# Residual of the delta inversion: b as two fp16 parts times the fp16 x, in place of fp32 b times a widened x

## The chip, the cores and the metric

The kernel runs on one core of a Trainium2 chip. The metric is the device time of one execution in microseconds. Three runs of the kernel before gave 3141.36, 3142.63 and 3150.59 us, so its median is 3142.63 us.

## The reference

One layer of a hybrid diffusion backbone over 1024 latent and 256 context tokens with 1024 channels: a modulation, a combined input projection, a bidirectional gated DeltaNet with 8 heads of 128 channels, a windowed attention, a merge of both branches, and a convolutional FFN. The change touches the DeltaNet alone. Its reference, cut to the part in question, is

```
gc = cumsum(g in the chunk)
decay = where(i >= j, exp(gc_i - gc_j), 0)
kk = k @ k.T
a_mat = where(i > j, beta_i * kk * decay, 0)
sol = triangular_solve(a_mat, [v * beta, k * beta * exp(gc)], lower=True, unit_diagonal=True)
```

and then a scan over the chunks. The solve is with the matrix I + a_mat. The kernel uses chunks of 128 tokens in place of 64, so each head has 10 chunks (8 latent, 2 of context) in 2 directions: 20 triangular matrices of 128x128.

## The kernel before, in words

`delta_net` runs 8 heads one after another. Every engine has its own program: a prologue, a loop over heads 0 to 6 with `fill` true, and the last head, written out with `fill` false. Nothing orders the engines but the counted semaphores (`Count`), and each engine takes its instructions in the order in which they are written.

A head goes through four stages:

- **Prepare** (`pe_prepare`, `act_body`, `dve_body`, `pool_body`). Tiles of two chunks in both directions (`bt` = 0 to 4, 128x512 numbers each) go through in turn: GpSimd masks g (`masked_g`), TensorE sums it and makes k @ k.T, ScalarE takes the exponential, VectorE multiplies into `bf` (b_full, fp32; L1666), GpSimd sets the diagonal of `bf` to 1 (L1806), and ScalarE rounds `bf` to fp16 as `b_h` (b_half, L1511). So b is I + a_mat in fp32, and b_h is its fp16 rounding.
- **Inversion** (`pe_inverse`, first loop). 7 levels of merging blocks of doubled size, 4 steps each, all in fp16: the products with `b_h` (L1303) are masked by VectorE with the level masks in `mats` (L1678, L1680) and give `x_h` (x_half), an approximate inverse, and `y_h` (y_half), its transpose.
- **Residual** (`pe_inverse`, second loop, L1343 to L1366). One refinement makes up for the fp16 of the inversion. For each `bt`, TensorE multiplies b with x in fp32: 4 matmuls of `bf` (L1351) with `x_f` (x_full), which is x_h widened to fp32 by GpSimd for bt 0, 2, 4 (L1819) and by ScalarE for bt 1, 3 (L1524). VectorE takes -2048 times the product plus 2048 times I as the fp16 residual `e_h` (L1692), TensorE multiplies it with y_h (4 matmuls, L1364), and VectorE adds 1/2048 of this to y_h and overwrites `bf` with it (L1700), which is the inverse that the chain uses. The residual tiles have two buffers. VectorE's order is e(0), e(1), inverse(0), e(2), inverse(1), e(3), inverse(2), e(4), inverse(3), inverse(4); TensorE's is product(0), product(1), second(0), product(2), second(1), and so on.
- **Chain** (`pe_chain`). The scan over 10 chunks, forward and backward. In heads 0 to 6, TensorE fills the waits between its small matmuls with the projections of the next head (`pe_group`, L1202), whose weight tiles GpSimd splits into a high and a low part (`pool_split`: L176 and L183).

GpSimd's order in a head: column copy (L1777), `masked_g` and `units`, five diagonals (L1806) with the other masks between them, the clearing of `o_acc` (L1812), two splits (the next head's k and v weights), the three widenings (L1819), then `pool_lines`, which waits for the end of the residual stage, and two more splits.

`decays` makes the columns of all heads in the prologue; `per_head` holds 6 kinds (`NK`) of 20 columns per head, which are copied to `col` at the start of a head. `x_f` lies over the first half of the region that held `conv_out`.

Of the kernel before, what the change touches and what calls it, by code (L numbers as in the profile page):

```python
# [15 lines left out]
P = 128  # L16
# [50 lines left out]
def constants():  # L67
    r, c = np.arange(P)[:, None], np.arange(P)[None, :]
    rot = np.zeros((P, P), np.float32)
    for base in (0, 64):  # L70
        for d in range(32):
            rot[base + 32 + d, base + d] = -1.0
            rot[base + d, base + 32 + d] = 1.0
    mats = [r == c, r >= 0, rot, c < r, c > r, c <= r, c >= r, NEG * (c < r), NEG * (c > r)]
    for level in range(LEVELS):
        s = 1 << level
        m = (r // (2 * s) == c // (2 * s)) & ((r // s) % 2 == 1) & ((c // s) % 2 == 0)
        unit = 1.0 * (r == c) if level == 0 else 0.0
        even = (np.arange(P) // s) % 2 == 0
        mats.append(np.concatenate([(unit - m)[:, even], (unit - m.T)[:, ~even]], 1))  # L80
    mats = np.stack([np.broadcast_to(m, (P, P)) for m in mats], 1).astype(np.float32)
    inv_freq = (np.float32(10000.0) ** (-np.arange(32, dtype=np.float32) / np.float32(32))).astype(np.float32)
    t = np.arange(SEQ)
    ang_r = (t // GRID_W).astype(np.float32)[None, :] * inv_freq[:, None]
    ang_c = (t % GRID_W).astype(np.float32)[None, :] * inv_freq[:, None]
    ang = np.concatenate([ang_r, ang_r, ang_c, ang_c], 0)
    return mats, np.stack([np.cos(ang), np.sin(ang)], 1).astype(np.float32)
# [878 lines left out]
K_G, K_BETA, K_EG, K_NEG_EG, K_BETA_REST, K_TOTAL = range(6)  # L966
NK = 6

def decays(core, per_head, at, ps, out):  # L970
# [50 lines left out]
    def vector_last(dve):  # L1021
        dve.wait_ge(s, 4)
        chain(dve, dve.tensor_tensor(ex[:, :, 1, :], ex[:, :, 1, :], beta[:, :, :], ALU.mult))
        chain(dve, dve.tensor_scalar(m[:, :, :], ex[:, :, 0, :], -1.0, None, ALU.mult))
        for kind, src in ((K_G, g[:, :, :]), (K_BETA, beta[:, :, :]), (K_EG, ex[:, :, 0, :]),
                          (K_NEG_EG, m[:, :, :]), (K_BETA_REST, ex[:, :, 1, :]), (K_TOTAL, ex[:, :, 2, :])):
            for di in range(2):
                dve.tensor_copy(per_head[:, :, kind, :, di].rearrange("p h c -> p c h"),
                                src[:, :, di * HEADS:(di + 1) * HEADS]).then_inc(out, 1)
        dve.wait_ge(out, 2 * NK)  # L1030

# [41 lines left out]
E_SCALE = 2048.0  # L1073
# [9 lines left out]
def delta_net(core, d):  # L1083
# [5 lines left out]
    with ExitStack() as st:  # L1089
# [38 lines left out]
        x_f = place("x_full", [P, NCH, 2, P], 0, F32)  # L1128
# [36 lines left out]
        xev, yac, xfa, osq = C("x_copied"), C("y_copied_act"), C("x_widened_act"), C("o_std")  # L1165
# [9 lines left out]
        xfp, unit = C("x_widened_pool"), C("x_and_y_units")  # L1175
# [92 lines left out]
        def pe_inverse(pe, h):  # L1268
# [73 lines left out]
            for bt in range(BT + 1):  # L1342
                if bt < BT:  # L1343
                    if bt % 2:
                        xfa.wait(pe, h * 2 + bt // 2 + 1)
                    else:
                        xfp.wait(pe, h * 3 + bt // 2 + 1)
                    ed.wait(pe, h * 5 + bt - 1)
                    for m in range(4):
                        c, di = 2 * bt + m // 2, m % 2  # L1350
                        mm = pe.matmul(bank[4 + bt % 2][:, m * P:(m + 1) * P], bf[:, c, di, :],  # L1351
                                       x_f[:, c, di, :], start=True, stop=True)
                    mm.then_inc(rd_.sem, 1)
# [139 lines left out]
        def act_body(act, h, fill):  # L1493
# [28 lines left out]
            xev.wait(act, h * MSTEPS + MSTEPS)  # L1522
            for bt in (1, 3):
                act.activation(flat(x_f, bt), flat(x_h, bt), ACT.Copy).then_inc(xfa.sem, 1)  # L1524
# [15 lines left out]
        def scalar(act):  # L1540
            for c in (evac, sil, sqd, stdc, tka, kqc, dct, bhd, xev, yac, xfa, osq):
                c.open(act)
# [109 lines left out]
        def dve_body(dve, h, fill):  # L1652
# [5 lines left out]
            for bt in range(BT):  # L1658
# [5 lines left out]
                for n in range(4):  # L1664
                    c, di = 2 * bt + n // 2, n % 2
                    ins = dve.scalar_tensor_tensor(out=bf[:, c, di, :], in0=bank[6 + bt % 2][:, (n // 2) * P:(n // 2 + 1) * P],  # L1666
                                                   scalar=col[:, K_BETA, c, di:di + 1], in1=dec[bt % 2][:, n // 2, di, :],
# [18 lines left out]
            for bt in range(BT + 1):  # L1686
                if bt < BT:
# [6 lines left out]
                                             scalar=-E_SCALE, in1=id_e[:, :].unsqueeze(1).broadcast_to([P, 4, P]),  # L1694
# [79 lines left out]
        def pool_body(pool, h, fill):  # L1774
# [28 lines left out]
            for bt in range(BT):  # L1803
                bqd.wait(pool, h * 5 + bt + 1)
                pool.sem_inc(turns, 1)
                pool.affine_select(flat(bf, bt), flat(bf, bt), pattern=[[0, 4], [1, P]], compare_op=ALU.not_equal,  # L1806
                                   fill=1.0, base=0, channel_multiplier=-1).then_inc(bfd.sem, 1)
                if bt + 2 < BT:
                    masked_g(bt + 2)
            pool.wait_ge(ystored, h * 16 + 16)  # L1810
# [5 lines left out]
            for bt in (0, 2, 4):  # L1816
                xev.wait(pool, h * MSTEPS + MSTEPS - (2 if bt == 0 else 0))
                pool.sem_inc(turns, 1)
                pool.tensor_copy(flat(x_f, bt), flat(x_h, bt)).then_inc(xfp.sem, 1)  # L1819
# [6 lines left out]
        def gpsimd(pool):  # L1826
            for c in (colc, tapc, padz, bfd, gld, dgd, xfp, unit, oz):
# [488 lines left out]
```

## Time and profile before

| | |
|---|---|
| median of three runs | 3142.63 us |
| the profiled execution | 3137.65 us, of which its span is 3135.8 us |
| TensorE matmuls busy | 2777.6 us (89% of the span) |
| VectorE busy | 1459.5 us (47%) |
| ScalarE busy | 775.3 us (25%) |
| GpSimd busy | 676.8 us (22%) |
| mean granted TensorE clock | 0.916 |
| the eight heads of the DeltaNet | from about 908 us to 2060 us of the span |

### The profile page before, as it was taken

How to read it: one execution, taken by the hardware profiler on the slowest of the kernel's cores; microseconds unless marked ns; L12 is line 12 of the kernel's file. 1: busy time of each engine (PE TensorE's matmuls, PEld its weight loads, DVE VectorE, ACT ScalarE, POOL GpSimd, SP SyncE). 2: the span in 40 equal slices, each digit the busy share in tenths (PEclk: the TensorE clock that was granted, in tenths of full speed). 3: DMA queues.
4: the chain of work that ended last, by engine and by line, in shares of the span. 5: the costliest groups of instructions: out<-in, count | busy, mean ns of one | idle time of the engine just before them, and what ended most of it. 6: DMA issues, size and time to landing. Idle time of an engine off the chain costs nothing. (4 is left out here: it accounts for less than half of the span.)

```text
span 3135.8 us, 45853 instructions
## 1 busy us (share of the span) xinstructions
PE 2777.6 (89%) x16872; PEld 2333.4 (74%) x16872; DVE 1459.5 (47%) x2531; ACT 775.3 (25%) x1386; POOL 676.8 (22%) x505
## 2 busy tenths in 40 slices
PE   8599999899889897988889897699686999997999
PEld 7476888778778786877778786578465888886877
DVE  1474444310436666656656666522114555555232
ACT  1421333210132514233242514110113121122010
POOL 0242000033231312122231312033112333331111
PEclk7799988899979899999989898799797999998999
DMA  4110112131100101000000100132321111111433
GB/s 190 56 33 7 61 67 95 73 109 66 54 8 7 35 1 36 14 23 22 15 28 8 35 1 8 66 116 87 121 100 47 47 53 47 47 47 60 127 124 98
DMA packets 41783, 175.69 MB, mean 56 GB/s; under 512 B 4624, under 2 KB 4880, under 8 KB 39696
## 3 DMA queue, kind: packets, MB, share of 16 engines
q1 hardware_dynamic: 39312, 169.19, 15.5%
q10 hardware_dynamic: 2304, 4.20, 0.3%
q8 instruction: 114, 1.87, 0.2%
q14 instruction: 53, 0.43, 0.0%
HBM read 148.20 MB, written 25.17 MB: 55 GB/s over the span
## 5 line engine op out<-in xcount | busy, mean ns | idle before, releaser
L193 PE MATMUL ps_up<-h_hi,up_w_hi 128*128 128x512 f32 x704 | 274.7, 390 | 37.4 <-POOL up_w_lo L183 37.4
L194 PE MATMUL ps_up<-h_lo,up_w_hi 128*128 128x512 f32 x704 | 274.4, 390 | 0.0
L195 PE MATMUL ps_up<-h_hi,up_w_lo 128*128 128x512 f32 x704 | 274.3, 390 | 0.0
L1202 PE MATMUL dn_bank<-h_hi,dn_w_hi 128*128 128x512 f32 (+1 forms) x640 | 245.4, 384 | 12.4 <-POOL dn_w_lo L183 12.4
L1202 PE MATMUL dn_bank<-h_hi,dn_w_lo 128*128 128x512 f32 (+1 forms) x640 | 245.7, 384 | 0.0
L1202 PE MATMUL dn_bank<-h_lo,dn_w_hi 128*128 128x512 f32 (+1 forms) x640 | 245.1, 383 | 0.0
L2072 DVE TENSOR_SCALAR ffn_u<-ffn_pad,vectors 128x1024 f32<-128x1024 f32 x44 | 105.3, 2394 | 230.7 <-ACT ffn_pad L2052 230.7
L193 PEld LDWEIGHTS ps_up<-h_hi,up_w_hi 128*128 128x128 f32 x704 | 132.5, 188 | 65.9 <-issue 38.2
L2141 PE MATMUL ps_down<-act_hi,down_w_hi 128*128 128x512 f32 x352 | 139.1, 395 | 24.5 <-DVE act_lo L2180 24.5
L194 PEld LDWEIGHTS ps_up<-h_lo,up_w_hi 128*128 128x128 f32 x704 | 132.6, 188 | 27.5
L195 PEld LDWEIGHTS ps_up<-h_hi,up_w_lo 128*128 128x128 f32 x704 | 132.4, 188 | 27.5
L1567 DVE SCALAR_TENSOR_TENSOR conv_out<-conv_in,head_taps,conv_out 128x1284 f32<-128x1284 f32 (+1 forms) x96 | 148.2, 1544 | 0.4
L1202 PEld LDWEIGHTS dn_bank<-h_hi,dn_w_hi 128*128 128x128 f32 x640 | 122.6, 192 | 29.7 <-POOL dn_w_lo L183 12.8
L1454 ACT ACTIVATE conv_in<-dn_bank 128x512 f32<-128x512 f32 (+1 forms) x64 | 34.9, 545 | 427.5 <-PE dn_bank L1202 421.3
L2142 PE MATMUL ps_down<-act_lo,down_w_hi 128*128 128x512 f32 x352 | 138.8, 394 | 0.0
L2143 PE MATMUL ps_down<-act_hi,down_w_lo 128*128 128x512 f32 x352 | 138.4, 393 | 0.0
L1202 PEld LDWEIGHTS dn_bank<-h_lo,dn_w_hi 128*128 128x128 f32 x640 | 122.7, 192 | 17.2
L1202 PEld LDWEIGHTS dn_bank<-h_hi,dn_w_lo 128*128 128x128 f32 x640 | 122.5, 191 | 17.0
L183 DVE TENSOR_TENSOR down_w_lo<-down_w_raw,down_w_hi 128x1408 fp32r<-128x1408 f32 x32 | 52.1, 1627 | 161.2 <-POOL down_w_hi L176 161.2
L176 POOL CAST up_w_hi<-up_w_raw 128x1024 fp32r<-128x1024 f32 x44 | 45.7, 1039 | 371.4 <-PE ps_up L195 311.3
L2076 DVE SCALAR_TENSOR_TENSOR ffn_u<-ffn_pad,vectors,ffn_u 128x1024 f32<-128x1024 f32 x88 | 113.0, 1285 | 12.8 <-DVE ffn_u L2076 0.2
L2052 ACT ACTIVATE ffn_pad<-ps_up 128x1024 f32<-128x1024 f32 x44 | 45.3, 1029 | 285.0 <-PE ps_up L195 284.9
(313 smaller groups left out, 6726.1 us busy)
## 6 DMA issues: line engine op xcount, KB each, us to landing
up_w_raw<-in_w_up SPq DMA_DIRECT2D x44, 512.0 KB, 3.3
down_w_raw<-in_w_down SPq DMA_DIRECT2D x32, 704.0 KB, 4.2
late_w_ada<-in_w_ada SPq DMA_DIRECT2D x8, 2048.0 KB, 9.7
dn_w_raw<-in_w_dn SPq DMA_DIRECT2D x32, 512.0 KB, 3.4
w_ada<-in_w_ada SPq DMA_DIRECT2D x4, 2048.0 KB, 12.7
at_w_raw<-in_w_mg_at SPq DMA_DIRECT2D x16, 512.0 KB, 4.2
dnm_w_raw<-in_w_mg_dn SPq DMA_DIRECT2D x16, 512.0 KB, 5.4
x_in<-in_xT SPq DMA_DIRECT2D x8, 640.0 KB, 10.0
```

The source lines that it names most:

```text
L176: pool.tensor_copy(self.hi[j][:, :, :], self.raw[j][:, :, :]).then_inc(self.hi_made, 1)
L183: eng.tensor_tensor(self.lo[j][:, :, :], self.raw[j][:, :, :], self.hi[j][:, :, :].bitcast(F32), ALU.subtract).then_inc(self.split, 1)
L193: pe.matmul(out, self.hi[j][:, k, :], xh, start=(k == 0), stop=False)
L194: pe.matmul(out, self.hi[j][:, k, :], xl, start=False, stop=False)
L195: mm = pe.matmul(out, self.lo[j][:, k, :], xh, start=False, stop=(k == self.kt - 1))
L1202: mm = pe.matmul(bank[4 + s % 3][:, 0:n], wt[:, k, :], x[:, k, t0:t0 + n], start=(k == 0 and v == 0), stop=(k == KT - 1 and v == 2))
L1567: ins = dve.scalar_tensor_tensor(out=dst, in0=src[:, j:j + n], scalar=taps[:, tile_at(tile), j:j + 1], in1=dst, op0=ALU.mult, op1=ALU.add)
L2072: ins = dve.tensor_scalar(u[:, s, :], src, tap(0), vec[:, bass.ds(m + s * FT + V_CONVB, 1)], ALU.mult, ALU.add)
L2076: ins = dve.scalar_tensor_tensor(out=u[:, s, :], in0=src, scalar=tap(n), in1=u[:, s, :], op0=ALU.mult, op1=ALU.add)
L2141: pe.matmul(ps[j][:, :], w.hi[part][:, k, :], hi, start=(kk == 0), stop=False)
L2142: pe.matmul(ps[j][:, :], w.hi[part][:, k, :], lo, start=False, stop=False)
L2143: mm = pe.matmul(ps[j][:, :], w.lo[part][:, k, :], hi, start=False, stop=(kk == FT - 1))
```

## The change

The fp32 product of the residual is replaced by two fp16 products that are added up in PSUM. b is scaled by 2048 (`E_SCALE`) as it is made: `decays` adds a seventh kind of column, `K_BETA_E` = 2048 beta, L1666 uses it in place of beta, and GpSimd sets the diagonal to 2048. `b_h` is then the fp16 rounding of the scaled b, and a new tile `b_l` (b_rest_half) holds in fp16 what the rounding left; GpSimd makes it by a subtraction for each `bt`, after the five diagonals and ahead of the clearing of `o_acc`. The level masks are divided by 2048, so that the inversion yields the same x and y. TensorE multiplies `b_h` and `b_l` with `x_h` (8 matmuls in fp16 for each `bt`, where 4 in fp32 were), and the factor of the residual on VectorE is -1 in place of -2048. `x_f` and its five widenings are gone.

```diff
-        mats.append(np.concatenate([(unit - m)[:, even], (unit - m.T)[:, ~even]], 1))
+        mats.append(np.concatenate([(unit - m)[:, even], (unit - m.T)[:, ~even]], 1) / E_SCALE)
...
-NK = 6
+K_G, K_BETA, K_EG, K_NEG_EG, K_BETA_REST, K_TOTAL, K_BETA_E = range(7)
+NK = 7
+E_SCALE = 2048.0
...
+        chain(dve, dve.tensor_scalar(e[:, :, :], beta[:, :, :], E_SCALE, None, ALU.mult))
         for kind, src in ((K_G, g[:, :, :]), (K_BETA, beta[:, :, :]), (K_EG, ex[:, :, 0, :]),
-                          (K_NEG_EG, m[:, :, :]), (K_BETA_REST, ex[:, :, 1, :]), (K_TOTAL, ex[:, :, 2, :])):
+                          (K_NEG_EG, m[:, :, :]), (K_BETA_REST, ex[:, :, 1, :]), (K_TOTAL, ex[:, :, 2, :]),
+                          (K_BETA_E, e[:, :, :])):
...
-        x_f = place("x_full", [P, NCH, 2, P], 0, F32)
+        b_l = place("b_rest_half", [P, NCH, 2, P], 0, F16)
...
-                    if bt % 2:
-                        xfa.wait(pe, h * 2 + bt // 2 + 1)
-                    else:
-                        xfp.wait(pe, h * 3 + bt // 2 + 1)
+                    xev.wait(pe, h * MSTEPS + MSTEPS - (2 if bt < 2 else 0))
+                    bld.wait(pe, h * 5 + bt + 1)
                     ed.wait(pe, h * 5 + bt - 1)
                     for m in range(4):
                         c, di = 2 * bt + m // 2, m % 2
-                        mm = pe.matmul(bank[4 + bt % 2][:, m * P:(m + 1) * P], bf[:, c, di, :],
-                                       x_f[:, c, di, :], start=True, stop=True)
+                        pe.matmul(bank[4 + bt % 2][:, m * P:(m + 1) * P], b_h[:, c, di, :],
+                                  x_h[:, c, di, :], start=True, stop=False)
+                        mm = pe.matmul(bank[4 + bt % 2][:, m * P:(m + 1) * P], b_l[:, c, di, :],
+                                       x_h[:, c, di, :], start=False, stop=True)
...
-            xev.wait(act, h * MSTEPS + MSTEPS)
-            for bt in (1, 3):
-                act.activation(flat(x_f, bt), flat(x_h, bt), ACT.Copy).then_inc(xfa.sem, 1)
...
-                                                   scalar=col[:, K_BETA, c, di:di + 1], in1=dec[bt % 2][:, n // 2, di, :],
+                                                   scalar=col[:, K_BETA_E, c, di:di + 1], in1=dec[bt % 2][:, n // 2, di, :],
...
-                                             scalar=-E_SCALE, in1=id_e[:, :].unsqueeze(1).broadcast_to([P, 4, P]),
+                                             scalar=-1.0, in1=id_e[:, :].unsqueeze(1).broadcast_to([P, 4, P]),
...
-                                   fill=1.0, base=0, channel_multiplier=-1).then_inc(bfd.sem, 1)
+                                   fill=E_SCALE, base=0, channel_multiplier=-1).then_inc(bfd.sem, 1)
...
+            kqc.wait(pool, h + 1)
+            for bt in range(BT):
+                bhd.wait(pool, h * 5 + bt + 1)
+                pool.sem_inc(turns, 1)
+                pool.tensor_tensor(flat(b_l, bt), flat(bf, bt), flat(b_h, bt), ALU.subtract).then_inc(bld.sem, 1)
...
-            for bt in (0, 2, 4):
-                xev.wait(pool, h * MSTEPS + MSTEPS - (2 if bt == 0 else 0))
-                pool.sem_inc(turns, 1)
-                pool.tensor_copy(flat(x_f, bt), flat(x_h, bt)).then_inc(xfp.sem, 1)
```

GpSimd's rows from the last two diagonals of a head to the first rows that follow the residual stage, before (dn_w_hi and dn_w_lo are the split weights, L1761 belongs to `pool_lines`):

```order
L1806 AFFINE_SELECT b_full<-b_full 128x512
L1810 ISA
L1812 MEMSET o_acc 128x1024
...
L176 CAST dn_w_hi<-dn_w_raw_4609 128x1024
...
L183 TENSOR_TENSOR dn_w_lo<-dn_w_raw_4609,dn_w_hi 128x1024
...
L176 CAST dn_w_hi<-dn_w_raw_4610 128x1024
...
L183 TENSOR_TENSOR dn_w_lo<-dn_w_raw_4610,dn_w_hi 128x1024
...
L1819 CAST x_full<-x_half 128x512
...
L1819 CAST x_full<-x_half 128x512 x2
```

The same place of the changed kernel:

```order
L1805 AFFINE_SELECT b_full<-b_full 128x512
L1813 TENSOR_TENSOR b_rest_half<-b_full,b_half 128x512 x5
L1814 ISA
L1816 MEMSET o_acc 128x1024
...
L176 CAST dn_w_hi<-dn_w_raw_4609 128x1024
...
L183 TENSOR_TENSOR dn_w_lo<-dn_w_raw_4609,dn_w_hi 128x1024
...
L176 CAST dn_w_hi<-dn_w_raw_4610 128x1024
...
L183 TENSOR_TENSOR dn_w_lo<-dn_w_raw_4610,dn_w_hi 128x1024
```

Five subtractions stand ahead of the clearing and of both splits; the three widenings behind the splits are gone.

TensorE's rows at the start of the residual stage of a head in the loop, before (the first line is the end of the inversion):

```order
L1332 MATMUL dn_bank<-identity_half,x_half 128x64 x10
L129 REGISTER_ALU
L1351 MATMUL dn_bank<-x_full,b_full 128x128 x4
L129 REGISTER_ALU
L1351 MATMUL dn_bank<-x_full,b_full 128x128 x4
L129 REGISTER_ALU
L1364 MATMUL dn_bank<-y_half,residual_half 128x128 x4
```

The same place of the changed kernel; the pair of its second and third rows comes eight times:

```order
L1334 MATMUL dn_bank<-identity_half,x_half 128x64 x10
L1351 MATMUL dn_bank<-x_half,b_half 128x128
L1353 MATMUL dn_bank<-x_half,b_rest_half 128x128
...
L129 REGISTER_ALU
L1366 MATMUL dn_bank<-y_half,residual_half 128x128 x4
```

8 fp32 matmuls became 16 in fp16, and two register operations ahead of the products are gone, since the waits need fewer computed values.

## Rows read from the trace of the kernel before

**Rows 1.** The page's first part: busy us, share of the span, instructions.

```profile
PE 2777.6 (89%) x16872; PEld 2333.4 (74%) x16872; DVE 1459.5 (47%) x2531; ACT 775.3 (25%) x1386; POOL 676.8 (22%) x505
```

**Rows 2.** Stretches: length; busy us of PE, PEld, DVE, ACT, POOL; PEclk; DMA share; GB/s.

```profile
955.05:963.30 8.25, 6.31 (x60) 5.77 (x60) 6.92 (x13) 0.67 (x2) 0.64 (x2) 1.00 0.01 2
1104.00:1165.00 61.00, 60.38 (x368) 53.62 (x369) 36.87 (x100) 10.85 (x14) 7.19 (x8) 0.99 0.00 1
```

**Rows 3.** Timeline, residual stage of head 1: start us, us, engine, line, operation [idle before].

```profile
1095.63 2.02 PE L1351 MATMUL dn_bank<-x_full,b_full 128*128 128x128 f32 x16
...
1096.96 0.69 DVE L1692 SCALAR_TENSOR_TENSOR residual_half<-dn_bank,identity_e_scale 128x512 f16<-128x512 f32 x1 [0.71 <-PE dn_bank L1351]
1097.84 0.69 DVE L1692 SCALAR_TENSOR_TENSOR residual_half<-dn_bank,identity_e_scale 128x512 f16<-128x512 f32 x1 [0.19 <-PE dn_bank L1351]
...
1097.99 0.38 PE L1364 MATMUL dn_bank<-y_half,residual_half 128*128 128x128 f16 x4 [0.35 <-DVE residual_half L1692]
...
1098.45 0.68 DVE L1700 SCALAR_TENSOR_TENSOR b_full<-dn_bank,y_half 128x512 f32<-128x512 f32 x1
...
1099.42 0.69 DVE L1692 SCALAR_TENSOR_TENSOR residual_half<-dn_bank,identity_e_scale 128x512 f16<-128x512 f32 x1 [0.29 <-issue]
1100.03 0.68 DVE L1700 SCALAR_TENSOR_TENSOR b_full<-dn_bank,y_half 128x512 f32<-128x512 f32 x1
...
1102.42 1.28 DVE L1700 SCALAR_TENSOR_TENSOR b_full<-dn_bank,y_half 128x512 f32<-128x512 f32 x2
...
1103.89 0.71 PE L1376 MATMUL dn_bank<-state,k_t 128*128 128x128 f32 x4 [0.94 <-DVE state L1608]
...
1104.36 0.48 PE L1202 MATMUL dn_bank<-h_hi,dn_w_hi 128*128 128x512 f32 x1
```

**Rows 4.** The same, first and last rows of head 4, and rows of head 7.

```profile
1519.18 2.02 PE L1351 MATMUL dn_bank<-x_full,b_full 128*128 128x128 f32 x16
...
1526.14 1.28 DVE L1700 SCALAR_TENSOR_TENSOR b_full<-dn_bank,y_half 128x512 f32<-128x512 f32 x2
...
1946.10 2.03 PE L1351 MATMUL dn_bank<-x_full,b_full 128*128 128x128 f32 x16
...
1947.34 0.69 DVE L1692 SCALAR_TENSOR_TENSOR residual_half<-dn_bank,identity_e_scale 128x512 f16<-128x512 f32 x1 [0.55 <-PE dn_bank L1351]
...
1952.52 1.27 DVE L1700 SCALAR_TENSOR_TENSOR b_full<-dn_bank,y_half 128x512 f32<-128x512 f32 x2
```

**Rows 5.** Groups by shape, 800 to 2000 us: busy us, mean ns | idle before.

```profile
L183 POOL TENSOR_TENSOR dn_w_lo<-dn_w_raw,dn_w_hi 128x1024 fp32r<-128x1024 f32 x32 | 77.0, 2407 | 2.6
...
L1786 POOL TENSOR_TENSOR g_masked<-constants,head_columns 128x512 f32<-128x512 f32 x40 | 41.2, 1039 | 1.4 <-POOL head_columns L1777 1.4
...
L1364 PE MATMUL dn_bank<-y_half,residual_half 128*128 128x128 f16 x160 | 15.5, 219 | 8.1 <-DVE residual_half L1692 8.1
```

**Rows 6.** Timeline, GpSimd in head 1: last diagonal, last split, first widening.

```profile
1071.75 0.63 POOL L1806 TENSOR_SCALAR_AFFINE_SELECT b_full<-b_full 128x512 f32<-128x512 f32 x1 [2.32 <-DVE b_full L1666]
...
1077.76 2.36 POOL L183 TENSOR_TENSOR dn_w_lo<-dn_w_raw,dn_w_hi 128x1024 fp32r<-128x1024 f32 x1
...
1093.64 0.61 POOL L1819 CAST x_full<-x_half 128x512 f32<-128x512 f16 x1 [13.53 <-ACT x_half L1516]
```

**Rows 7.** Timeline, VectorE in the prologue: columns of the decays.

```profile
908.52 0.24 DVE L1024 TENSOR_SCALAR decay_m<-decay_exps 128x160 f32<-128x160 f32 x1
...
909.69 0.57 DVE L1028 COPY per_head_columns<-decay_exps 128x80 f32<-128x80 f32 x4
```

**Rows 8.** Stretches in head 1 (first three) and head 7, columns as in rows 2.

```profile
1071.39:1074.80 3.41, 1.76 (x40) 1.42 (x40) 2.31 (x6) 1.17 (x2) 2.96 (x4) 1.00 0.00 0
1074.80:1078.21 3.41, 3.15 (x49) 2.75 (x48) 2.34 (x6) 1.53 (x4) 3.33 (x3) 0.50 0.13 29
1100.50:1103.90 3.40, 1.79 (x21) 1.44 (x18) 3.40 (x8) 0.00 (x0) 0.00 (x0) 1.00 0.00 0
1955.43:1972.50 17.07, 15.74 (x58) 13.00 (x58) 9.77 (x33) 0.00 (x0) 0.00 (x0) 0.50 0.01 1
```

More of the change, by code:

```diff
@@ L962, in attention @@
     merge_stage(core, "at", core.y_dram, d["w_mg_at"], core.merged_dram)
-K_G, K_BETA, K_EG, K_NEG_EG, K_BETA_REST, K_TOTAL = range(6)
-NK = 6
+K_G, K_BETA, K_EG, K_NEG_EG, K_BETA_REST, K_TOTAL, K_BETA_E = range(7)
+NK = 7
+E_SCALE = 2048.0
 def decays(core, per_head, at, ps, out):
@@ L1072 @@
 YHALF = STEPS // 2
-E_SCALE = 2048.0
 ORDER = [list(range(XCH, NCH)) + list(range(XCH)), list(range(NCH - 1, XCH - 1, -1)) + list(range(XCH - 1, -1, -1))]
@@ L1164, in delta_net @@
         tka, kqc, dct, bhd = C("tok_act"), C("kq_copied"), C("decay"), C("b_rounded")
-        xev, yac, xfa, osq = C("x_copied"), C("y_copied_act"), C("x_widened_act"), C("o_std")
+        xev, yac, osq = C("x_copied"), C("y_copied_act"), C("o_std")
         qsd, ovr = C("q_sums_copied"), C("o_var")
@@ L1174, in delta_net @@
         colc, tapc, padz, bfd, oz = C("columns"), C("taps"), C("pad_zeroed"), C("b_with_i"), C("o_zeroed")
-        xfp, unit = C("x_widened_pool"), C("x_and_y_units")
+        bld, unit = C("b_rest"), C("x_and_y_units")
         gld, dgd = C("g_masked"), C("k_rstd_diag")
@@ L1540, in scalar @@
         def scalar(act):
-            for c in (evac, sil, sqd, stdc, tka, kqc, dct, bhd, xev, yac, xfa, osq):
+            for c in (evac, sil, sqd, stdc, tka, kqc, dct, bhd, xev, yac, osq):
                 c.open(act)
@@ L1826, in gpsimd @@
         def gpsimd(pool):
-            for c in (colc, tapc, padz, bfd, gld, dgd, xfp, unit, oz):
+            for c in (colc, tapc, padz, bfd, gld, dgd, bld, unit, oz):
                 c.open(pool)
```

## The prediction

> **What bounds the kernel now.** I began with the page's first part: TensorE's matmuls are busy for 89% of the span, every other engine for less than half [rows 1]. The change touches one stage of each of eight heads, so the next view is the stretches around it. In the chain, which takes about 61 of a head's 141 us (heads 1 to 4 start their stages at 1095.63 and 1519.18), TensorE is busy for 60.38 of 61.00 us at a granted clock of 0.99: it is the bound there, and whatever the stage ahead of it saves reaches the end in full, since the chain's first matmul waits for the last inverse. In the residual stage nothing is full: PE 6.31, VectorE 6.92 of 8.25 us, ScalarE and GpSimd next to nothing, clock 1.00 [rows 2]; the other seven stages are alike.
>
> The timeline of one such stage shows who waits for whom [rows 3]. TensorE starts product(0) and product(1), 16 records, at 1095.63. VectorE's e(0) starts 1.33 us later, e(1) at 1097.84. e(0) is over at 1097.65, and second(0) starts 0.34 us after that; inverse(0) starts 0.46 us behind second(0). e(2) at 1099.42 is still late. From there VectorE starts an operation every 0.60 or 0.61 us (1099.42, 1100.03), ends at 1103.70 and waits for nothing. So the stage has two parts: a start in which VectorE waits for fp32 products, and a steady part of 0.60 us per VectorE operation, which TensorE doesn't set. From 1095.63 to 1103.70 it is 8.07 us. Five heads (0, 1, 3, 5, 6) have this length within 0.01 us, heads 2 and 4 have 8.22 and 8.24, since second(0) starts 0.16 us later there, and the last has 7.69 [rows 4].
>
> **The change part by part.** *The products.* Before: 16 records in 2.02 us; with 0.22 us for a matmul by itself [rows 5] that is (2.02 - 0.22) / 15 = 0.12 us each, and product(0), 8 records, is done 7 x 0.12 + 0.22 = 1.06 us after its start. e(0) follows 0.27 us later (1.33 - 1.06). After: also 8 matmuls, in fp16. Four such matmuls (second(0)) take 0.38 us [rows 3], one takes 0.219 [rows 5], so they follow each other by (0.38 - 0.22) / 3 = 0.054 us. product(0) is done after 7 x 0.054 + 0.22 = 0.60, and e(0) starts at 0.60 + 0.27 = 0.87 us. Then, from the start of the stage: e(1) at 1.47 (product(1) is done at 1.03); e(0) over at 1.56; second(0) at 1.90; inverse(0) at 2.36. product(2) is issued 0.22 us behind the start of second(0), at 2.12, and allows e(2) at 2.99. Six more starts of 0.60 (inverse 1, e 3, inverse 2, e 4, inverse 3, inverse 4) give 6.59, and the last lasts 0.68: 7.27 us. That is 0.80 us less than 8.07. Heads 2 and 4 keep their 0.16 us, so they save the same; the last head begins e(0) at 1.24 - 0.46 = 0.78, has a short wait for second(0) and comes to 6.86 for 7.69, 0.83 less. Sum: 8 x 0.80 = 6.5 us saved. Although TensorE's work on the products falls by half (5 x 8 x (0.12 - 0.054) = 2.6 us a head), only 0.8 of it is on the path: the rest stands beside VectorE's 0.60 us steps.
>
> The trace has no chain of fp16 matmuls that alternates two weights into one PSUM bank. Bounds: if they went at the fp32 records' 0.12 us, nothing is saved; if every wait of VectorE in the start vanished, the stage would be 0.87 + 9 x 0.60 + 0.68 = 6.95 us, 1.12 us a head, 9 us in all. I take 6.5, near the upper end, because second(0) is the same shape and type. The Trainium skill (TensorE: Matmul & The Clock Gate, Back-to-back issue gap) gives about 81 ns per load-and-matmul pair at 128 columns; by it the products would be done 0.2 us later in each head and the sum would be 4.9 instead of 6.5, while the row has 54.
>
> *The widenings.* Five casts of some 0.6 us on two engines go. TensorE waited for none of them: GpSimd's first ran at 1093.64 [rows 6], two microseconds ahead of product(0), which itself follows the end of the inversion. Nothing is saved. The waits in their place (last x_half, rest made) are older still; two register operations ahead of the products go and one wait is added: 0, with 0.05 us a head either way.
>
> *The subtractions on GpSimd.* Five of 128x512, which no row shows. g_masked, 128x512 from two inputs, takes 1.04 us; the split's 128x1024 takes 2.41, or 1.2 us for half [rows 5]. I take 1.1 each, 5.5 us; between nearly nothing (0.6 each, as the casts) and 2.4 each, 12 us. They start behind the last diagonal and its rounding, at about 1072.9, so the rests are ready by 1079 (by 1085 at worst), and product(0) comes at 1095. Queued behind them: the clearing of o_acc and two splits, which ended at 1080.12 and will end at 1085.6 (1092 at worst); the chain's first use of those weights is at 1104.36 [rows 3]. GpSimd idled 13.53 us there [rows 6]. Cost: nothing; the idle stretch is the cover, and beyond 24 us of subtractions it would be gone. They now run beside the inversion's masks on VectorE, as the splits did already.
>
> *The prologue.* One more 128x160 operation, 0.24 us, and two more copies of 0.57 / 4 = 0.14 us [rows 7], 0.5 us once, ahead of GpSimd's first column copy, with TensorE's transposes beside it: between 0 and 0.5, I take 0.2. The column copy of each head grows by a sixth, beside transposes too: 0. VectorE's other operations change a constant only.
>
> *The clock.* This is the term that I can't read off. TensorE does less in the stage: per tile 8 x 0.12 + 4 x 0.054 = 1.18 us of matmuls before, 12 x 0.054 = 0.65 after; over the stage 5.9 of 8.07 us (73%) becomes 3.2 of 7.27 (45%). Granted clock falls in this kernel where TensorE is thinly occupied though never idle for long: in head 1, after 3.41 us with 1.76 busy, it was 0.50 for 3.41 us; the last 3.40 us of the residual stage had 1.79 busy, mostly fp32 columns, and the clock held [rows 8]. In the last head, whose chain has no filling work, it fell right behind the stage and stayed at 0.50 for 17 us. So the residual stage is near the edge, and its second half (one product, two seconds and the wait for the last inverse) goes down to less than such stretches had. A fall comes a little after, when TensorE should run the chain's dense matmuls. A stretch of 3.41 us at 1.2 instead of 2.4 GHz costs half of itself, 1.7 us, if all of it is dense; some of it will lie over the end of the stage, and I take 1.3. Where the stage lies against these spells differs from head to head, so I expect it in four of the seven filled heads: 4 x 1.3 = 5.2 us given back, with ends 0 and 7 x 1.7 = 12.
>
> The Trainium skill, same page, What's actually happening, says that the "default state is throttled, and activity releases the throttle", and its account of kernels that lose the clock is of waits with an idle TensorE. The change adds no such wait, and by that account the clock would hold; the rows of this case show falls without idleness.
>
> Sum: -6.5 + 0.2 + 5.2 = -1.1 us on 3137.65, the profiled execution. That execution is 5 us under the median of 3142.63; on the median it gives 3141.5 us.
>
> **The rivals.** *The clock holds* in all heads. For it: it held in all eight stages before; against it: rows 8. Then -6.5 + 0.2 = -6.3, 3136.3 us.
>
> *The clock falls in every filled head*, at the chain's start: slower than before. For it: the thin second half of the stage; against it: the spells don't begin at the same point of every head. 7 x 1.7 = 12 against 6.3 saved: +5.6, 3148.2 us. It decides from 5 heads at 1.3 us on; beyond +9.4 us it would need second spells behind the first, for which the dense chain leaves little room.
>
> *The products aren't what VectorE waits for*, or the alternating weights slow the fp16 matmuls to the fp32 pace: the change doesn't do what it says for the time. Against it: the 0.71 us that VectorE idles before e(0) ends with L1351. Then 0 to +0.5, 3142.9 us.
>
> **How the numbers follow.** Forecast 0.45, clock holds 0.30, clock falls everywhere 0.13, no gain 0.12. About 0.3% (9.4 us) is what a measurement of this kernel can tell from no change, and all four lie inside it: the largest saving that I can build is 9 us, the largest loss 6. Faster by more than 0.3% needs the upper bound or luck with spells elsewhere in the heads, whose places all shift: 0.12. Slower by more than 0.3%: 0.07. Within: 0.81. Range: from the clock that holds with a little more, 3133, to the fall in every head, 3149; the three runs of before are themselves 9 us apart.
>
> **What would show it.** The residual stage from first product to last inverse: 7.27 us in heads 0, 1, 3, 5, 6, with e(0) at 0.87 and VectorE's starts 0.60 apart from e(2) on. b_rest_half about 1.1 us each, over well before the stage, and no wait of PE for POOL. PEclk in the 4 us behind the stage: 0.50 for a spell in about four of heads 0 to 6. Wrong would be: a stage of over 7.6 us; no spell in any head, or one in all seven; a wait for a split at the chain's start; longer masks (L1680) on VectorE beside the subtractions.

## The result: 0.3% slower, outside the predicted range

| | before | changed |
|---|---|---|
| median of 5 runs each | 3142.08 us (3138.76 to 3150.59) | 3153.18 us (3147.00 to 3157.43) |
| ratio, 95% interval | | 1.003 (1.0016 to 1.0044) |
| profiled execution, its span | 3137.65, 3135.8 us | 3147.00, 3145.2 us |

Forecast were 3141.5 us and a range of 3133 to 3149. A second measurement of the same changed kernel (12 runs, 20 of before) gave 3153.19 against 3146.58, 1.0017 (1.0007 to 1.0028): slower again, by 6.6 us. The two intervals together put the loss between 2 and 14 us.

The page's first part of the changed kernel, as in [rows 1]. TensorE's busy time fell by only 2 us: by 17 in the eight residual stages (50.5 to 33.5), while in the chains it rose by 11 (591.7 to 602.7), where the same matmuls ran at a lower clock. GpSimd's rose by 29.

```profile
PE 2775.5 (88%) x16872; PEld 2325.2 (74%) x16872; DVE 1459.5 (46%) x2534; ACT 767.6 (24%) x1370; POOL 705.5 (22%) x521
```

The residual stage of head 1 from the first product on, and 61 us of its chain (columns as in [rows 2]). The stage was 8.07 us and is 7.15; TensorE's busy time in it was 6.31 and is 4.20, and its clock held. In the chain TensorE is busy for the same 60.38 us, but at a mean clock of 0.97 where it was 0.99.

```profile
1097.21:1104.36 7.15, 4.20 (x63) 3.36 (x60) 6.66 (x12) 0.00 (x0) 0.00 (x0) 1.00 0.01 2
1105.00:1166.00 61.00, 60.38 (x363) 53.40 (x362) 35.59 (x99) 9.38 (x12) 6.86 (x4) 0.97 0.00 1
```

The timeline of that stage: TensorE's first two products (start us, us), VectorE's operations, and the matmuls behind them. They answer to [rows 3].

```profile
1097.21 0.22 PE L1351 MATMUL dn_bank<-x_half,b_half 128*128 128x128 f16 x1
1097.27 0.22 PE L1353 MATMUL dn_bank<-x_half,b_rest_half 128*128 128x128 f16 x1
```
```profile
1098.02 1.29 DVE L1691 SCALAR_TENSOR_TENSOR residual_half<-dn_bank,identity_e_scale 128x512 f16<-128x512 f32 x2 [0.20 <-PE dn_bank L1353]
1099.48 0.69 DVE L1699 SCALAR_TENSOR_TENSOR b_full<-dn_bank,y_half 128x512 f32<-128x512 f32 x1 [0.17 <-PE dn_bank L1366]
1100.09 0.68 DVE L1691 SCALAR_TENSOR_TENSOR residual_half<-dn_bank,identity_e_scale 128x512 f16<-128x512 f32 x1
...
1103.07 1.28 DVE L1699 SCALAR_TENSOR_TENSOR b_full<-dn_bank,y_half 128x512 f32<-128x512 f32 x2
```
```profile
1099.06 0.38 PE L1366 MATMUL dn_bank<-y_half,residual_half 128*128 128x128 f16 x4 [0.79 <-DVE residual_half L1691]
...
1103.22 0.40 PE L1366 MATMUL dn_bank<-y_half,residual_half 128*128 128x128 f16 x4 [0.80 <-DVE residual_half L1691]
1104.55 0.60 PE L1378 MATMUL dn_bank<-state,k_t 128*128 128x128 f32 x3 [0.94 <-DVE state L1607]
```

e(0) starts 0.81 us behind the first product (1098.02 - 1097.21), against 1.33 before; from e(2) at 1100.09 on VectorE runs back to back. The wait in front of e(0) has gone from 0.71 to 0.20 us.

GpSimd in head 1, to set beside [rows 6]: the five subtractions are over at 1079.71, the second split at 1087.45, and GpSimd then idles for 17 us. Forecast were 1079 and 1085.6, the split being 1.9 us later than that without anybody waiting; 1.6 us of it is that the whole head lies later (first product 1097.21 instead of 1095.63). Behind the prologue, which has two copies and one operation more [rows 7], head 0's column copy begins at 912.36 instead of 910.68.

```profile
1074.09 5.62 POOL L1813 TENSOR_TENSOR b_rest_half<-b_full,b_half 128x512 f16<-128x512 f32 x5
...
1085.08 2.37 POOL L183 TENSOR_TENSOR dn_w_lo<-dn_w_raw,dn_w_hi 128x1024 fp32r<-128x1024 f32 x1
1104.59 0.18 POOL L1760 MEMSET conv_in<- 128x4 f32 x3 [17.14 <-DVE b_full L1699]
```

**Where the time went.** I divided each head at four marks: GpSimd's column copy, VectorE's first x_half, the first product, the end of the last inverse. "Filled" heads are heads 0 to 6, whose chains hold projections of the next head. A fall is a change of the granted clock from 1.00 to 0.50 (2.4 to 1.2 GHz), and a spell is the time it stays there. "Low" is the time at a granted clock of 0.50, worked out for each stretch as twice its length times (1 - PEclk). Sums over eight heads of the profiled executions, us:

| | to first x_half (low) | to product(0) (low) | residual stage | chain (low) | end of head 7 |
|---|---|---|---|---|---|
| before | 198.4 (82) | 189.5 (30) | 64.5 | 643.3 (68) | 2006.4 |
| changed | 200.6 (90) | 189.7 (30) | 56.8 | 655.2 (91) | 2014.6 |
| changed, again | 198.3 (88) | 191.1 (37) | 57.3 | 660.5 (107) | 2026.5 |

The residual stage gave back 7.7 us. The chain, whose instructions the change doesn't touch, took 11.9 more: 13.4 more in the filled heads, 1.5 less in the last (52.58 to 51.04). The part to the first x_half took 2.2 more, the way to the first head 1.7, the inversion 0.2. Together -7.7 + 11.9 + 2.2 + 1.7 + 0.2 = 8.3 of the span's 9.4 us.

The chain's loss stands in the clock. These are the 10 us behind the residual stage, heads 0 to 7 of the changed kernel, then heads 0 and 1 of before, where all seven filled heads read 1.00 (length; busy us of PE, PEld, DVE, ACT, POOL; PEclk; DMA share; GB/s):

```profile
963.67:973.67 10.00, 9.80 (x53) 8.38 (x54) 3.28 (x14) 0.60 (x1) 0.37 (x4) 1.00 0.01 2
1104.36:1114.36 10.00, 9.81 (x44) 8.31 (x45) 3.23 (x12) 0.60 (x1) 0.37 (x4) 0.83 0.01 2
1246.24:1256.24 10.00, 9.82 (x36) 8.25 (x37) 2.70 (x10) 0.00 (x0) 0.37 (x4) 0.68 0.01 2
1389.60:1399.60 10.00, 9.83 (x36) 8.27 (x37) 2.69 (x10) 0.00 (x0) 0.37 (x4) 0.68 0.01 2
1532.70:1542.70 10.00, 9.81 (x45) 8.39 (x46) 3.32 (x12) 0.60 (x1) 0.38 (x4) 0.84 0.01 2
...
1963.00:1973.00 10.00, 8.30 (x31) 6.68 (x31) 6.51 (x21) 0.00 (x0) 0.00 (x0) 0.65 0.00 0
```
```profile
963.12:973.12 10.00, 9.80 (x53) 8.42 (x54) 3.33 (x14) 0.60 (x1) 0.37 (x4) 1.00 0.01 2
1103.70:1113.70 10.00, 9.81 (x53) 8.46 (x54) 3.35 (x13) 0.60 (x1) 0.37 (x4) 1.00 0.01 2
```

PEclk 0.83 over 10 us is 3.4 us at 1.2 GHz, 0.68 is 6.4 us. Six of seven filled heads have a fall there, two of them a double one (the spell lasts twice as long): 3.4 + 6.4 + 6.4 + 3.2 + 3.4 + 3.0 = 25.8 us low, of which half is lost where TensorE is the bound: up to 12.9 us. In head 2 the timeline of TensorE and the stretches show it record by record:

```profile
1245.21 0.28 PE L1366 MATMUL dn_bank<-y_half,residual_half 128*128 128x128 f16 x2
1246.42 1.23 PE L1378 MATMUL dn_bank<-state,k_t 128*128 128x128 f32 x4 [0.94 <-DVE state L1607]
...
1247.87 0.63 PE L1204 MATMUL dn_bank<-h_lo,dn_w_hi 128*128 128x512 f32 x1
1248.29 0.63 PE L1204 MATMUL dn_bank<-h_hi,dn_w_lo 128*128 128x512 f32 x1
```
```profile
1242.00:1245.40 3.40, 1.98 (x28) 1.37 (x25) 3.40 (x7) 0.00 (x0) 0.00 (x0) 1.00 0.02 5
1245.40:1248.80 3.40, 2.46 (x10) 2.09 (x9) 1.80 (x6) 0.00 (x0) 0.37 (x4) 0.55 0.00 0
1248.80:1252.20 3.40, 3.40 (x12) 2.82 (x11) 0.68 (x3) 0.00 (x0) 0.00 (x0) 0.50 0.00 0
1252.20:1255.60 3.40, 3.40 (x18) 2.82 (x17) 1.05 (x4) 0.00 (x0) 0.00 (x0) 0.95 0.00 0
```

The four fp32 matmuls that take 0.71 us in [rows 3] take 1.23 here, and the 512-column ones follow each other by 0.42 us (1248.29 - 1247.87) instead of 0.23. The clock goes to 0.50 while TensorE waits 0.94 us for the last inverse, and stays there through a whole stretch in which TensorE is busy for 3.40 of 3.40 us. Head 3 does the same, to the hundredth (1392.50 to 1395.90: busy 3.40, clock 0.50).

What TensorE did just before is in the last 3.40 us of head 1's stage, before and changed:

```profile
1100.30:1103.70 3.40, 1.98 (x22) 1.61 (x21) 3.40 (x7) 0.00 (x0) 0.00 (x0) 1.00 0.00 0
```
```profile
1100.96:1104.36 3.40, 1.50 (x20) 0.98 (x18) 3.40 (x7) 0.00 (x0) 0.00 (x0) 1.00 0.00 0
```

Its work there fell from 1.98 to 1.50 us, and its longest wait stayed at 0.94.

### The profile page after: what moved, and what is told of

Same layout as the page of the kernel before. It is cut to its first block and busy times, and to the rows that moved or that the text cites. A ratio compares the mean times of both kernels' runs of the same rounds, so it can differ in the third digit from the quotient of the medians.

```text
span 3145.2 us, 45851 instructions
## 1 busy us (share of the span) xinstructions
PE 2775.5 (88%) x16872; PEld 2325.2 (74%) x16872; DVE 1459.5 (46%) x2534; ACT 767.6 (24%) x1370; POOL 705.5 (22%) x521
## 6 DMA issues: line engine op xcount, KB each, us to landing
late_w_ada<-in_w_ada SPq DMA_DIRECT2D x8, 2048.0 KB, 10.5
```

## The experiments

Theory A: the clock's falls behind the stage cost what the chain lost, and they come because TensorE does too little in the stage. Rival B: the subtractions on GpSimd slow something. Rival C: the slower result is scatter between executions. In the diffs below lines of context are left out. Ratios are to the kernel before, measured together with each experiment, with 95% intervals.

**1. The changed kernel again, no edit.**

> The changed kernel as it is, on the chip and in the rounds of the next three. Both theories: 8 to 12 us slower than before, as measured. Its profile is a second look at where the granted clock falls: in the first one TensorE's clock was at 0.50 over the start of the chain in six of the seven filled heads (twice for some 6.8 us instead of 3.4). If that belongs to the change, five or more of seven show it again; if it was chance, two to four do.

Measured: 3153.19 us (3147.99 to 3162.57), 1.0017 (1.0007 to 1.0028), 6.6 us by the medians where 8 to 12 was expected. The clock fell behind the stage in seven of seven filled heads, in two of them twice. Heads 0, 1 and 3 of its trace, in the 10 us behind the stage:

```profile
970.60:980.60 10.00, 9.80 (x36) 8.26 (x37) 2.72 (x11) 0.00 (x0) 0.37 (x4) 0.69 0.01 2
1113.72:1123.72 10.00, 9.81 (x45) 8.38 (x46) 3.32 (x12) 0.60 (x1) 0.37 (x4) 0.84 0.01 2
...
1400.60:1410.60 10.00, 9.81 (x36) 8.28 (x37) 2.72 (x10) 0.00 (x0) 0.38 (x4) 0.68 0.00 0
```

Rival C falls: both measurements are slower and the falls repeat.

**2. and 3. Idle matmuls in the residual stage of the changed kernel.** They write a PSUM bank that nobody reads then; the result is unchanged. Number 2 issues 48 a head (8 behind each of products 1 to 4, at the last turn and at the end), number 3 only the 24 last of these.

```diff
+            def idle_work(k, end=False):
+                for i in range(k):
+                    a, b = (core.id_h[:, :],) * 2 if end else (b_h[:, i % 4, 0, :], x_h[:, i % 4, 0, :])
+                    pe.matmul(bank[3][:, (i % 4) * P:(i % 4 + 1) * P], a, b, start=True, stop=True)
...
                     mm.then_inc(rd_.sem, 1)
+                    if bt in (4,):          # number 2: (1, 2, 3, 4)
+                        idle_work(8)
                 if bt >= 1:
+                    if bt == BT:
+                        idle_work(8)
...
                     mm.then_inc(y2d.sem, 1)
+            idle_work(8, end=True)
```

> The changed kernel with TensorE work that nobody reads: 48 fp16 matmuls per head into a free PSUM bank, 8 behind each of products 1 to 4, 8 ahead of the last second product and 8 behind it, in TensorE's waits for VectorE. That is 2.6 us a head, as much as the change took from TensorE. Theory A (the thinner residual stage makes the granted clock fall at the chain's start, and that is the loss): the clock holds there in all heads, the residual stage stays within 0.4 us of its 7.14 us, and the kernel is 4 to 8 us faster than before (ratio 0.9975 to 0.9987). Theory B (the loss comes from elsewhere: subtractions on GpSimd, prologue, a shift of the heads): it stays 8 us slower or gets slower still by the added work.

> As the one before, but only at the end of the stage: 8 idle matmuls behind product 4, 8 ahead of the last second product and 8 behind it, 24 per head. Theory A, if the last 3 us of the stage decide: as good as the one with 48, clock held in all or all but one head, 4 to 8 us faster than before. If the whole stage counts: spells in some heads, between the two. Theory B: 8 us slower as the changed kernel.

Measured: 3134.82 us, 0.9958 (0.9945 to 0.9972), and 3133.46 us, 0.9954 (0.994 to 0.9969). Work that computes nothing makes the changed kernel 18 and 20 us faster than it was when measured together with them (3153.19). Behind the stage no head of number 3 has a fall; heads 0, 1 and 7:

```profile
967.02:977.02 10.00, 9.80 (x53) 8.40 (x54) 3.31 (x14) 0.60 (x1) 0.37 (x4) 1.00 0.01 2
1107.45:1117.45 10.00, 9.80 (x53) 8.41 (x54) 3.29 (x14) 0.60 (x1) 0.37 (x4) 1.00 0.01 2
...
1951.10:1961.10 10.00, 8.50 (x45) 6.15 (x46) 7.41 (x25) 0.00 (x0) 0.00 (x0) 1.00 0.01 2
```

Its residual stages sum to 56.7 us, as in the changed kernel, and its chains to 635.5 (33 low) against 655.2 (91 low). Against before the stage gives 7.8 us and the last head's chain 5.6 (52.58 to 46.94): together 13.4; the rest of the heads about cancels (filled chains -2.3, the part to the first x_half +2.5, inversion -0.4). The medians differ by 13.1. The spans of the two profiled executions differ by 6.9 only: number 3's is 5.1 us longer ahead of the heads (first column copy at 915.77 instead of 910.68) and 1.4 behind them. So theory A accounts for what the changed kernel had lost: against it number 3 differs in the idle matmuls alone, its stage is as long, and its chains are 19.7 us shorter. It is more than I had expected, since the last head gains as well.

**4. Less work still.** Only the product with b's high part is left; b's low part is missing from the residual.

```diff
-                        pe.matmul(bank[4 + bt % 2][:, m * P:(m + 1) * P], b_h[:, c, di, :],
-                                  x_h[:, c, di, :], start=True, stop=False)
-                        mm = pe.matmul(bank[4 + bt % 2][:, m * P:(m + 1) * P], b_l[:, c, di, :],
-                                       x_h[:, c, di, :], start=False, stop=True)
+                        mm = pe.matmul(bank[4 + bt % 2][:, m * P:(m + 1) * P], b_h[:, c, di, :],
+                                       x_h[:, c, di, :], start=True, stop=True)
```

> The changed kernel without the matmuls with b_rest_half (4 fp16 matmuls a tile in place of 8; the residual then lacks b's low part); the subtractions on GpSimd stay. TensorE does still less in the stage. Theory A: the stage is 0.2 to 0.3 us shorter a head, and the clock falls at the chain's start in all seven filled heads, more often for two spells: 0 to 5 us slower than the changed kernel though work was taken out. Theory B: 2 us faster than the changed kernel.

Measured: 3156.09 us, 1.0024 (1.001 to 1.0038). The stages sum to 55.4 us, another 1.4 less, and the chains to 661.5 (110 low), with a fall behind the stage in all seven filled heads, three of them double. A kernel with 160 matmuls fewer isn't faster: here too less work in the stage goes with a longer low clock behind it. The 2.9 us by which it is slower than number 1 are within the scatter of either (3148 to 3163).

**5. Rival B: the kernel before with the five subtractions added.** Their result isn't used, but the widenings, which overwrite it, wait for them.

```diff
+            bld.wait(act, h * 5 + 5)
...
+            kqc.wait(pool, h + 1)
+            for bt in range(BT):
+                bhd.wait(pool, h * 5 + bt + 1)
+                pool.sem_inc(turns, 1)
+                pool.tensor_tensor(flat(b_l, bt), flat(bf, bt), flat(b_h, bt), ALU.subtract).then_inc(bld.sem, 1)
...
+            bld.wait(pool, h * 5 + 5)
```

> The kernel before with nothing but the five subtractions on GpSimd, b_full - b_half, at the place where the changed kernel has them (into the region of x_full, which is overwritten later; here the result is used by nobody). If GpSimd's added 5.6 us per head cost nothing, as predicted, the ratio is 1.000 within 0.0015. If they are behind the loss (late splits, VectorE's masks slowed beside them), 5 to 10 us slower.

Measured: 3146.73 us, 1.0004 (0.9995 to 1.0013). They are the size they have in the changed kernel, in the group of the trace:

```profile
L1816 POOL TENSOR_TENSOR b_rest_half<-b_full,b_half 128x512 f16<-128x512 f32 x40 | 45.0, 1158 | 0.0
```

They cost nothing that shows (+1.3 us by the ratio, interval -1.6 to +4.1). Rival B falls: numbers 2 and 3 keep the subtractions and are faster than before.

**6. and 7. Useful work in the stage instead.** Matmuls of the next head's first projection move out of the chain into TensorE's waits in the residual stage: 6 of its 24 in the kernel before, 13 in the changed one. Bank 6, free there, holds that projection.

```diff
+        EARLY = {2: (0, 2), 3: (2, 4), 4: (4, 6), 5: (6, 9), 'end': (9, 13)}
+        LATE = [(13, 17), (17, 21), (21, 24)]
...
                 if bt >= 1:
+                    early(bt)
...
+            early("end")
```

> The kernel before with part of the next head's first projection group moved into TensorE's waits at the end of the residual stage: 2 of its 24 matmuls (0.23 us each at full clock) ahead of the last second product, 4 behind it; the group goes to PSUM bank 6. TensorE waits 0.67 and 0.94 us there. Expected: 6 x 0.23 = 1.4 us a filled head off the chain, 7 x 1.4 = 9 us, ratio 0.997; the clock held there before and holds now.

> The changed kernel with 13 of those 24 matmuls in TensorE's waits of the residual stage: 2 behind each of products 2, 3 and 4, 3 ahead of the last second product, 4 behind it. Theory A: the clock holds at the chain's start of the seven filled heads, as with idle work (12 us faster than before), and up to 13 x 0.23 = 3.0 us a head is taken off the chain, of which I expect 1.5 to 2.5 us: 10 to 18 us more, ratio to before 0.990 to 0.993. If the moved matmuls only delay the stage, the gain is that of the idle work, 0.9955.

Measured: 3133.15 us, 0.9956 (0.9943 to 0.9968), and 3126.94 us, 0.9933 (0.992 to 0.9946). Number 6 gave 13 us where 9 were expected. Number 7 gave 19 in all, 6.6 more by the ratios than idle work (number 3) where 10 to 18 more were expected, and its 0.9933 lies just outside the 0.990 to 0.993. In number 7 the stage is longer (7.57 us in a filled head, where 7.14 was), which takes back part of the 13 matmuls; behind it the clock holds in heads 0 to 6. The last head has nothing to move in, and its clock falls (heads 0 and 7):

```profile
969.88:979.88 10.00, 10.00 (x56) 8.51 (x55) 5.05 (x19) 0.60 (x1) 0.37 (x4) 1.00 0.01 2
...
1942.85:1952.85 10.00, 8.85 (x32) 7.10 (x32) 6.27 (x23) 0.00 (x0) 0.00 (x0) 0.59 0.00 0
```

**8. The idle matmuls of number 3 in the kernel before.**

> The kernel before with the 24 idle fp16 matmuls per head at the end of its residual stage. There the clock fell behind the stage in the last head only, so the idle work has little to hold up: within 3 us of before, ratio 0.999 to 1.001, or 2 to 4 us less if it helps the last head. If idle work makes any version faster by 10 us, it isn't the change's own thinness that was mended in the other runs.

Measured: 3143.98 us (3130.3 to 3149.54), 0.9992 (0.9983 to 1.0001). The profiled execution was the fastest of its 11, so its trace says little of the median. Idle work is worth little where the clock holds in seven heads anyway; that its last head should have gained 5.6 us isn't seen in the median, which fell by 2.4. It also shows what the change is worth where both kernels have the same idle work: 3133.46 us (number 3) against 3143.98, and by the ratios 12 us. The heads of the two traces differ by 6.6 us (1082.3 and 1088.8), near the 6.3 forecast for a clock that holds; that is one pair of executions.

**9. and 12. Idle matmuls behind products 1 to 3**, 24 a head, and none behind product 4 or at the end. Number 12 is a second trace of the same kernel. The diff is against number 3.

```diff
-                    if bt in (4,):
+                    if bt in (1, 2, 3):
                         idle_work(8)
-                    if bt == BT:
-                        idle_work(8)
-            idle_work(8, end=True)
```

> The changed kernel with the same 24 idle fp16 matmuls per head as in the run with idle work at the end, but behind products 1, 2 and 3, and none in the last third of the stage. If the end of the stage decides (theory A in its narrow form), the clock still falls at the chain's start in four to seven filled heads and the kernel is no more than 4 us faster than the changed one. If it is the amount of TensorE's work over the whole stage, it is as good as the run with idle work at the end: 12 us faster than before.

> A second profile of the version with 24 idle matmuls behind products 1, 2 and 3. In the first, the clock held behind the stage in all seven filled heads and fell for 9.6 us in the last, though the median of its runs was 8 us above that of the version with idle work at the end. If the end of the stage decides, this look shows one to four spells behind the stage of the filled heads; if the amount over the whole stage does, none again.

Measured: 3141.66 us, 0.9989 (0.9979 to 0.9999); the one run of number 12 took 3141.58. I had expected it to fall in one to seven filled heads if the end of the stage decides, and 12 us less than before if the whole stage does. Neither came: in none of the filled heads of both traces does the clock fall behind the stage, in both it falls in the last head, and number 9 gains 3 to 4 us on before. Heads 0 and 7 of number 9:

```profile
968.71:978.71 10.00, 9.80 (x53) 8.38 (x54) 3.28 (x14) 0.60 (x1) 0.37 (x4) 1.00 0.01 2
...
1957.31:1967.31 10.00, 9.24 (x30) 7.38 (x31) 6.04 (x21) 0.00 (x0) 0.00 (x0) 0.52 0.01 2
```

Against number 3 its last chain is 54.57 us instead of 46.94, its stages sum to 57.7 instead of 56.7, and its other chains to 590.5 instead of 588.5: 7.6 + 1.0 + 1.9 = 10.5 us, and the ratios stand 11 us apart (0.0035 of 3146). So 24 idle matmuls behind products 1 to 3 were enough for the clock of the filled heads but not of the last; in the five traces with idle work at the end of the last head's stage (numbers 2, 3, 8, 10 and 11) it didn't fall there.

Number 9 doesn't settle whether the end or the whole stage counts, since its end isn't left as thin as it was. The matmuls behind product 3 run from 1105.76 to 1106.37 in head 1, and TensorE is busy for 1.86 of the stage's last 3.40 us, against 1.50 in the changed kernel and 1.98 before:

```profile
1105.87:1109.27 3.40, 1.86 (x29) 1.44 (x26) 3.40 (x7) 0.00 (x0) 0.00 (x0) 1.00 0.00 0
```

**10. Eight idle matmuls at the very end only**, with `idle_work` as in number 3.

```diff
                     mm.then_inc(y2d.sem, 1)
+            idle_work(8, end=True)
```

> The changed kernel with 8 idle matmuls per head only, behind the last second product, in the 0.94 us in which TensorE waits for the last inverse. If this gap is what counts: as fast as with 24. If TensorE's work over the last few microseconds counts, 0.43 us isn't enough for all positions: spells in one to four heads, 2 to 9 us faster than the changed kernel.

Measured: 3133.98 us, 0.9962 (0.995 to 0.9973), with one fall in seven filled heads (head 6) and none in the last. Eight matmuls, 0.056 us apart, are enough for nearly all of it.

Taken together: in the three traces with the change and no idle or moved work (changed, 1 and 4) the clock fell behind the stage in 6, 7 and 7 of seven filled heads; in the seven with the change and such work (2, 3, 7, 9, 10, 11 and 12) in 0, 0, 0, 0, 1, 0 and 0. The idle matmuls are fp16, so it isn't the loss of fp32 work as such.

**11. Number 7 with the 24 idle matmuls in the last head.**

```diff
+                elif not fill and slot in (4, 5, "end"):
+                    for i in range(8):
+                        a, b = (core.id_h[:, :],) * 2 if slot == "end" else (b_h[:, i % 4, 0, :], x_h[:, i % 4, 0, :])
+                        pe.matmul(bank[3][:, (i % 4) * P:(i % 4 + 1) * P], a, b, start=True, stop=True)
```

> The changed kernel with 13 projection matmuls moved into the residual stage of the filled heads (19 us faster than before when run alone) and, in the last head, which has no projection to move, 24 idle matmuls at the stage's end. In the profile of the run without them the last head's chain had the clock at 0.50 for 33 of 55 us, with idle work in two other runs for 5 to 8 of 47. Expected: 3 to 8 us faster than without, ratio to before 0.991 to 0.993; within 1 us of it if the fall in the last head comes from the chain itself.

Measured: 3122.90 us (3119.97 to 3125.55), 0.9927 (0.9914 to 0.994), the fastest of all: 23 us under before. By the ratios (0.9927 and 0.9933) that is only 2 us better than number 7, with intervals that overlap, where 3 to 8 were expected; in the traces the last head's chain is 5.2 us shorter. Its last head, where number 7 had 0.59:

```profile
1940.36:1950.36 10.00, 8.51 (x45) 6.17 (x46) 7.40 (x25) 0.00 (x0) 0.00 (x0) 1.00 0.01 2
```

## Why the prediction was wrong

- **Length of the stage: right.** Forecast 7.27 us, measured 7.14 in all seven filled heads and 6.78 (forecast 6.86) in the last: 7.7 us saved for 6.5. Heads 2 and 4 didn't keep their extra 0.16 us (8.22 and 8.24 before); in number 1 heads 3, 4 and 5 had it (7.30). The sixteen fp16 matmuls follow each other by 0.056 us (1097.21 to 1098.05 from first to last), near the 0.054 worked out from second(0); the 81 ns that the Trainium skill gives (TensorE: Matmul & The Clock Gate, Back-to-back issue gap) doesn't show in the trace, which goes by the row. e(0) came at 0.81 us (0.87 forecast), VectorE's steps were 0.60.
- **GpSimd and the widenings: right.** 1.16 us a subtraction (1.1 taken), over 17 us before the stage, and by experiment 5 without a cost that shows.
- **Prologue: at the upper end.** 0.2 forecast, with 0.5 as the end of its range. From the operation ahead of the added ones (decay_m, 908.52 and 909.70) to the first column copy (910.68 and 912.36) it is 2.16 us before and 2.66 changed: 0.5. The other 1.2 us of the 1.7 lie ahead of anything that was added, and there executions scatter: the first column copy is at 910.3 to 920.5 in the four traces with the old prologue, and at 912.2 to 919.4 in the ten with the new one.
- **The clock: the step that failed.** It said: "I expect it in four of the seven filled heads: 4 x 1.3 = 5.2 us given back". In the two executions there were falls in six and in seven heads, 25.8 and 28.8 us low, up to 12.9 and 14.4 us given back. Both factors were too small.
- **Its number of heads** was taken from the idea that "where the stage lies against these spells differs from head to head"; it does in before (column copies 140.2 to 142.8 us apart), but from head 2 on those of the changed kernel are 143.2 to 143.5 us apart, and the falls come at nearly the same place of each. That equal periods do this is my reading of the two traces, not tested; that like falls make the heads equally long is as possible.
- **Its price** was taken for one spell, and the rival's bound, "it would need second spells behind the first, for which the dense chain leaves little room", is what the traces of heads 2 and 3 refute: the second stretch was low with TensorE busy all through it. With the measured terms, -7.7 + 12.9 = +5.2 us on this profile. The other 4.2 of its +9.4 are about 2.2 ahead of the first x_half (8 us more low), 1.7 before the first head, 0.2 in the inversion and 1.2 behind the heads, less 1.0 that the chains lost less than 12.9.
- **The mechanism of the clock** was foreseen, also that it is the end of the stage that gets thin ("its second half ... goes down to less than such stretches had"); the estimate of TensorE's share in the stage, 73% to 45%, was by matmul spacing, and by busy time it is 6.31 of 8.07 us to 4.19 of 7.14, 78% to 59%.
- **The rival "falls in every filled head"** had the right mechanism and sign, with 0.13 for its chance, and was priced at 1.7 us a head, where the double spells make it 1.8 to 2.1 (12.9 and 14.4 over seven). Its +5.6 us is close to the +6.6 of the second measurement. Its chance should have been higher: [rows 8] had a fall after a stretch with 1.76 of 3.41 us busy, and the stage's end went to 1.50 of 3.40.
- **The Trainium skill's account** (same page, What's actually happening: "the default state is throttled, and activity releases the throttle"). The traces agree as to activity: in number 10 eight more matmuls keep the clock that fell without them. I read the account as one of waits alone and so as speaking for a clock that holds. That was too narrow a reading, since the same page of the Trainium skill also tells of short idling between groups of matmuls that costs the clock (A second HAM failure mode: psum-queue depth-cycling). Here TensorE's longest wait in the stage stayed at 0.94 us, as before, only its work was thinner, and the clock fell.

**What stays open.** Where a spell begins within a head, and why the chain's middle and late spells (68 us low in before with the last head's, 33 in number 3, 57 in number 10) vary from head to head, isn't settled; nor whether the last microseconds of the stage or all of it count; nor why number 8 gained so little, where its one trace has no fall behind any stage. Each kernel but the changed one and that of number 9 has one trace.

## What to carry to other kernels

Where TensorE waits for another engine just ahead of a stretch that it bounds, count what it still does in those waits before you make its work lighter: here 7.7 us saved in the stage cost up to 13 in the chains behind it. Fill the waits with work from the dense stretch (number 7), or, where there is none, with a few matmuls whose result nobody reads (number 10). And work a prediction's clock term out for every head, with one spell and with two: where the heads are equally long, as here, a fall in one can come in all.

## What the runs showed of the hardware

- Eight idle fp16 matmuls a head, 8 x 0.056 = 0.45 us, took the changed kernel from 0.2 or 0.3% slower than before to 0.4% faster, 17 to 21 us (number 10).
- After a thin stage the granted clock stayed at 1.2 GHz through 3.40 us in which TensorE was busy all the time, in two of seven heads (2 and 3 of the changed kernel); it was back at 2.4 GHz behind that.
- Removing 160 matmuls (number 4) made no time go away (3156.09 us for 3153.19), and 48 idle ones more a head (number 2) made the kernel faster by some 18 us (3153.19 to 3134.82); all three were measured together.
- Two fp16 matmuls with different weights that add up in one PSUM bank follow each other by 0.056 us, where an fp32 one of the same shape took two records of 0.12.
